# Later places for modulation rows, two retention chunk roundings, token-state remainders and the last Fourier fold

## The reference

```
mod = silu(c) @ w_ada + b_ada          # six rows of 1024: sh1, sc1, g1, sh2, sc2, g2
h   = rms_norm(x) * (1 + sc1) + sh1
u, q, k, v, g, ga, gb = split(h @ w_in)
y_four = real(fft2(u over positions and channels of 4 groups)) @ four_w_out
y_ret  = (silu(g) * group_norm(bidirectional_retention(q, k, v))) @ ret_w_out
y   = sigmoid(ga) * y_four + sigmoid(gb) * y_ret
x   = x + g1 * (y @ w_out)
h2  = rms_norm(x) * (1 + sc2) + sh2
x   = x + g2 * (square(relu(h2 @ w_mlp1)) @ w_mlp2)
out = rms_norm(x)
```

## Time and profile before

| | |
|---|---|
| median of 3 runs | 1274.28 us (1273.71 to 1274.79) |
| profiled execution, first to last instruction | 1273.3 us |
| PE busy (matmul) | 1247.7 us, 98% |
| DVE, ACT, POOL busy | 884.7, 610.2, 163.1 us |
| mean TensorE clock granted | 0.998 |

### The profile page before, as it was taken

One profiled execution on the slowest core, in us unless ns is written; L12 is line 12 of the kernel. 1 busy time (PEld: TensorE's weight loads), 2 busy tenths in 40 slices (PEclk: granted clock), 3 DMA queues, 4 the chain that ended last, 5 costly groups with the idle time before them and its releaser, 6 DMA issues.

```text
span 1273.3 us, 16935 instructions
## 1 busy us (share of the span) xinstructions
PE 1247.7 (98%) x6216; PEld 1030.8 (81%) x6216; DVE 884.7 (69%) x1392; ACT 610.2 (48%) x1039; POOL 163.1 (13%) x112
## 2 busy tenths in 40 slices
PE   5999999999999999999999999999999999999997
PEld 3788788888988878888888888888888888888886
DVE  5572577758659987877688665565555669768866
ACT  7761211235436433443677555555545433654444
POOL 0125330142260000025510000000000000000000
PEclk9999999999999999999999999999999999999999
DMA  9414220103276456496732644444448985477534
GB/s 368 181 33 154 78 100 2 34 20 100 69 274 230 141 202 211 161 365 234 265 133 88 200 166 143 149 164 142 140 156 281 320 292 183 159 236 256 193 105 160
DMA packets 95226, 219.18 MB, mean 172 GB/s; under 512 B 11532, under 2 KB 11932, under 8 KB 95144
## 3 DMA queue, kind: packets, MB, share of 16 engines
q1 hardware_dynamic: 82752, 182.70, 42.2%
q10 hardware_dynamic: 8728, 22.29, 4.7%
q0 software_dynamic: 3664, 13.11, 3.2%
HBM read 166.66 MB, written 51.39 MB: 171 GB/s over the span
## 4 chain that ended last, share of the span: by engine, by line
PE 81%; DVE 7%; DMA 6%; issue 2%; ACT 2%; POOL 1%; SPq 1%; ACTq 0%; DVEq 0%
PE ps L2988 13%; PE ps L2990 13%; PE ps L2989 13%; PE ps L3607 8%; PE ps L3599 8%; PE ps L3602 8%; DMA raw<-in_w_stream 3%; PE ps L3625 3%; PE ps L3437 3%; PE ps L3442 3%; PE ps L3439 3%; PE ps L3029 2%; PE ps L3071 1%; POOL ring_lo L1051 1%; PE ps L3224 1%
## 5 line engine op out<-in xcount | busy, mean ns | idle before, releaser
L2988 PE MATMUL ps<-t_hi,s_hi 128*128 128x512 f32 x392 | 153.4, 391 | 0.1
L2989 PE MATMUL ps<-t_lo,s_hi 128*128 128x512 f32 x392 | 153.1, 391 | 0.0
L2990 PE MATMUL ps<-t_hi,s_lo 128*128 128x512 f32 x392 | 153.1, 391 | 0.0
L1792 ACT ACTIVATE s_hi<-s_raw 128x512 fp32r<-128x512 f32 x112 | 70.5, 630 | 114.0 <-DMA b<-in_w_stream 58.4
L1051 POOL TENSOR_TENSOR ring_lo<-raw,ring_hi 128x1024 fp32r<-128x1024 f32 (+2 forms) x37 | 86.2, 2342 | 207.1 <-ACT ring_hi L1177 203.4
L2867 DVE TENSOR_TENSOR s_lo<-s_raw,s_hi 128x512 fp32r<-128x512 f32 x112 | 77.3, 690 | 42.3 <-ACT s_hi L1792 41.8
L2988 PE MATMUL ps<-ring_hi,hT_hi 128*128 128x512 f32 x224 | 91.4, 408 | 0.0
L2990 PE MATMUL ps<-ring_hi,hT_lo 128*128 128x512 f32 x224 | 87.7, 391 | 0.0
L2989 PE MATMUL ps<-ring_lo,hT_hi 128*128 128x512 f32 x224 | 87.5, 391 | 0.0
L2988 PEld LDWEIGHTS ps<-t_hi,s_hi 128*128 128x128 f32 x392 | 73.6, 188 | 16.2 <-DVE t_lo L2871 0.5
L2990 PEld LDWEIGHTS ps<-t_hi,s_lo 128*128 128x128 f32 x392 | 73.7, 188 | 15.9
(11 more groups left out here) (509 smaller groups left out, 3201.7 us busy)
## 6 DMA issues: line engine op xcount, KB each, us to landing
s_raw<-ff_scr SPq DMA_DIRECT2D x112, 256.0 KB, 2.8
raw<-in_w_stream SPq DMA_DIRECT2D x34, 512.0 KB, 3.9
ff_scr<-ffs SPq DMA_DIRECT2D x16, 1024.0 KB, 4.8
t_raw<-in_w_stream SPq DMA_DIRECT2D x64, 256.0 KB, 3.4
w_B_raw<-in_w_stream SPq DMA_DIRECT2D x48, 256.0 KB, 2.8
ff_scr<-ffa SPq DMA_DIRECT2D x16, 768.0 KB, 4.5
b<-in_w_stream SPq DMA_DIRECT2D x48, 256.0 KB, 4.5
ada_next<-in_ada_columns POOLq DMA_DIRECT2D x13, 512.0 KB, 3.8
```

Source lines behind the costliest of these rows:

```text
L1792: A(s_slot[n][0][:], s_slot[n][2][:], ACT.Copy).then_inc(down_hi, 1)
L2988: M(dst, lhsT=l_hi, rhs=r_hi, start=first, stop=False, skip_group_check=goes_on)
L2989: M(dst, lhsT=l_hi, rhs=r_lo, start=False, stop=False, skip_group_check=goes_on)
L2990: return M(dst, lhsT=l_lo, rhs=r_hi, start=False, stop=last, skip_group_check=goes_on)
```

## The change

Order and places change; no arithmetic does.

- PE: `ret_product(3)` comes before `fold(3)`. The wait of `parts(0)` for u chunk 3 moves to kt = 6. The 16 `xq` matmuls are no longer spread over the eight steps but follow the last step, in a new function `quarter_row`.
- DVE: the remainder of u chunk 3 comes behind `xq` and `operand_lo(0)` to `(2)`. `add_row(0)` and `add_row(1)` stand after the tiles m = 5 and 6, no longer 2 and 6. `add_row(7)` moves from the end of the step before j = 2 to behind `g_add("22", 2)`.
- ACT: `operand_hi(2)` comes before the rounding of u chunk 3. The load of row 1 is issued right behind that of row 0, into the second `yr_out` buffer. The roundings of re chunks 2 and 3 move from m = 3 and 4 to m = 5 and 6. The wait for both rows in front of `copy_half(8)` is split: row 0 there, row 1 in front of `copy_half(10)`.
- POOL: the two pieces of the token-state remainder (line 1116) come behind the remainders of all four "fo" chunks, no longer behind the second.

```diff
--- before.py
+++ after.py
@@ -326,7 +326,7 @@
         an = place("an", o_t + 10304, [P, 2 * EVEN - 2], F32R)
         yr_out = [place("yr_out0", o_t + 12384, [P, SEQ]), place("yr_out1", o_t + 16480, [P, SEQ])]
         gate_row = place("gate_row", o_t + 6144, [KT, P])
-        ada_first = [yr_out[0], yr_out[0], place("ada_first2", o_t + 6144, [P, D])]
+        ada_first = [yr_out[0], yr_out[1], place("ada_first2", o_t + 6144, [P, D])]
         ada_next = place("ada_next", o_qt + 12288, [P, D])
         ada_late = [place(f"ada_late{n}", o_v + 4096 * n, [P, D]) for n in range(3)] + [ada_next]
 
@@ -549,6 +549,8 @@
 
             if j == 0:
                 eng.wait_ge(dft_done, 4)
+            elif j == 1:
+                yr_stored(eng, 3)
             elif j < 18:
                 eng.wait_ge(mod_done, j)
             elif j < 21:
@@ -1108,14 +1110,14 @@
                 lo(i)
             pool.wait_ge(f_used, 10)
             nc.gpsimd.memset(wn_raw[:], 0.0).then_inc(cleared, 1)
-            for i in range(INDEX[("cs", 3)], INDEX[("fo", 2)]):
+            for i in range(INDEX[("cs", 3)], INDEX[("re", 2)]):
                 lo(i)
             pool.wait_ge(f_sum, 9)
             for n in range(2):
                 ks = slice(4 + 2 * n, 6 + 2 * n)
                 nc.gpsimd.tensor_tensor(hT_lo[:, ks, 0:512], h_raw[:, ks, 0:512], hT_hi[:, ks, 0:512].bitcast(F32),
                                         ALU.subtract).then_inc(h_whole, 1)
-            for i in range(INDEX[("fo", 2)], INDEX[("wo", 0)]):
+            for i in range(INDEX[("re", 2)], INDEX[("wo", 0)]):
                 lo(i)
             for j in range(3, 16):
                 load_ada(pool, j)
@@ -1406,9 +1408,9 @@
             operand_hi(0)
             copy_half(2)
             operand_hi(1)
+            operand_hi(2)
             hi_to(("u", 3))
-            for n in (2, 3):
-                operand_hi(n)
+            operand_hi(3)
             for r in (3, 4):
                 copy_half(r)
             for n in (4, 5):
@@ -1501,6 +1503,7 @@
             act.wait_ge(rows_stored, 16)
             act.dma_start(silu_row[:], silu_scr[0:1, :].to_broadcast([P, D])).then_inc(silu_in, 16)
             load_ada(act, 0)
+            load_ada(act, 1)
 
             def copy_b(m):
 
@@ -1519,11 +1522,9 @@
                     store_yf(m - 1)
                 if m in (1, 2):
                     hi_to(("fo", m + 1))
-                if m in (3, 4):
-                    hi_to(("re", m - 1))
-                if m == 3:
-                    load_ada(act, 1)
-            act.wait_ge(mod_done, 2)
+                if m in (5, 6):
+                    hi_to(("re", m - 3))
+            act.wait_ge(mod_done, 1)
             copy_half(8)
             store_yf(KT - 1)
             load_ada(act, 2)
@@ -1531,6 +1532,7 @@
             copy_half(9)
             g_his(1, ("B11",))
             g_his(0, ("T3", "T1"))
+            act.wait_ge(mod_done, 2)
             copy_half(10)
             g_s_hi("g1", g1_hi[:], g1_raw[:])
             g_his(1, ("T3", "T1"))
@@ -2325,12 +2327,13 @@
             even_operand(0, 1)
             for s_ in range(2):
                 even_operand(1, s_)
-            u_lo(3)
             do.chain(V.tensor_tensor(xq_raw[:, :, None], h_raw[:, :, 256:257], h_raw[:, :, 768:769], ALU.add))
             do.chain(V.tensor_copy(xq[:, :, 0:1], xq_raw[:, :, None]))
             V.tensor_tensor(xq[:, :, 1:2], xq_raw[:, :, None], xq[:, :, 0:1].bitcast(F32), ALU.subtract).then_inc(f_sum, 1)
-            for n in range(4):
+            for n in range(3):
                 operand_lo(n)
+            u_lo(3)
+            operand_lo(3)
 
             for half in range(2):
                 dve.wait_ge(f_used, 4 + half + 1)
@@ -2501,8 +2504,8 @@
                 do(V.tensor_copy(y[:, HALF:HALF + 1], ps[:, b, 256:257]))
                 do.chain(V.tensor_tensor(y[:, SEQ - 1:HALF:-2], ps[:, b + 1, 0:256], b_sb[:, 256:512], ALU.add),
                          four_free)
-                if m in (2, 6):
-                    add_row(m // 4)
+                if m in (5, 6):
+                    add_row(m - 5)
                 if m >= 6:
                     g_sums(m - 6, ("T3", "T1"))
 
@@ -2559,6 +2562,8 @@
             for j in range(1, KT - 3):
                 if j > 1:
                     g_add("22", j)
+                if j == 2:
+                    add_row(7)
                 g_los(j + 1, LATER_UNITS[2:])
                 if j < 3:
                     add_row((5, 8)[j - 1])
@@ -2570,7 +2575,8 @@
                 g_los(j + 2, LATER_UNITS[:2])
                 both_parts(j)
                 g_add("11", j + 1)
-                add_row(6 + 2 * j if j > 1 else 7)
+                if j > 1:
+                    add_row(6 + 2 * j)
             g_add("22", 5)
             g_los(6, LATER_UNITS[2:])
             g_add("12", 5)
@@ -3285,13 +3291,27 @@
             ret_product(1)
             fold(2)
             ret_product(2)
+            ret_product(3)
             fold(3)
-            ret_product(3)
             ret_product(4)
 
+            def quarter_row(cols_):
+
+                pe.wait_ge(f_sum, 5)
+                n_cols = GROUPS * (cols_.stop - cols_.start)
+                for kt in range(KT):
+                    w = slice(kt % 2 * 512, (kt % 2 + 1) * 512)
+                    for e, x in enumerate(chunk(("u", kt // 2))):
+                        r = x[:, w].rearrange("p (g d) -> p g d", g=GROUPS)[:, :, cols_]
+                        mm = M(ps[0:2, 5, 0:n_cols], lhsT=xq[:, kt, :], rhs=r, start=kt == 0 and e == 0,
+                               stop=kt == KT - 1 and e == 1)
+                return mm
+
             def parts(base, cols_, tiles):
 
                 for kt in range(KT):
+                    if kt == 6:
+                        pe.wait_ge(split, INDEX[("u", 3)] + 1)
                     w_hi, w_lo = chunk(("u", kt // 2))
                     w = slice(kt % 2 * 512, (kt % 2 + 1) * 512)
                     r_hi, r_lo = (x[:, w].rearrange("p (g d) -> p g d", g=GROUPS)[:, :, cols_] for x in (w_hi, w_lo))
@@ -3302,10 +3322,8 @@
                         l_hi, l_lo = e_operand(s_)
                         toks = slice(tile * P, (tile + 1) * P)
                         mm = mm3(ps[:, n, 0:n_cols], l_hi[:, kt, toks], l_lo[:, kt, toks], r_hi, r_lo, kt == 0, kt == KT - 1)
-                    if base == 0:
-                        pe.wait_ge(f_sum, 5)
-                        M(ps[0:2, 5, 0:n_cols], lhsT=xq[:, kt, :], rhs=r_hi, start=kt == 0, stop=False)
-                        mm = M(ps[0:2, 5, 0:n_cols], lhsT=xq[:, kt, :], rhs=r_lo, start=False, stop=kt == KT - 1)
+                    if kt == KT - 1 and base == 0:
+                        mm = quarter_row(cols_)
                     if kt % 4 == 3 or base and kt % 2 == 1:
                         mm.then_inc(f_used, 1)
 
@@ -3313,7 +3331,6 @@
             side_out(pe, ("rt", 7))
             for n in (6, 7):
                 main_read(pe, MIDX[("g", n)])
-            pe.wait_ge(split, INDEX[("u", 3)] + 1)
             parts(0, slice(0, FW), ((0, 0), (0, 1), (1, 0), (1, 1)))
             for r in (5, 6):
                 ret_product(r)
```

## The result

The changed kernel takes 1277.07 us at the median, against 1274.86 us for the kernel before on the same chip: ratio 1.0017, interval 1.0009 to 1.0024. On a second chip the two stood at 1275.75 and 1273.13 us, ratio 1.0019 (1.0010 to 1.0028). So the change costs 2.2 to 2.6 us. I had predicted a gain of 1.5 us and a range up to 1274.8. The profiled execution has a span of 1274.7 us.

The account below looks back on a forecast made before the run. PE, busy 98% of the span, was taken as the bound. Fold -1.14, Fourier -2.1, retention +0.2 and gate stage +1.5 gave -1.54 us: span 1271.8, plus 0.98 around it, 1272.7 us; range 1270.7 to 1274.8.

Parts of the forecast that it names:

- Bound and places: Whole kernel: PE busy 98% of the span; five places where it stands still hold together 5.0 us, the most to win.
- Fold and first parts: Before fold(3) and parts(0): waits for DVE remainders shrink, gain 1.14 us, bounds 0 and 1.26.
- Fourier products: Before four_product(5) and (6): both stalls go, gain 2.1 us; later retention products give back 0.2 us.
- The lock: DVE and POOL share a port pair exclusively; add_row(0) and (1) collide again with POOL's remainders, supporting the 0.2 us stall.
- Gate stage: Moving add_row(7): (3,2) gains 0.40 us, but later loads 8 and 9 delay (3,3); cost 1.5 us, bounds -0.4 and +4.
- Rival 2: Gate stage: loads 8 and 9 each land in 5.5 to 6 us, row 9 and (3,3) 4.8 us late; 1276.0 us, chance 0.09.
- Sum: Whole kernel: -1.14 - 2.1 + 0.2 + 1.5 = -1.54 us on the span, 1271.8, plus 0.98: 1272.7 us.
- Rival 1: Gate stage: the load chain absorbs the delay, row 9 late by 0.5 us or less; about 1271.2 us, chance 0.24.
- Rival 3: Early stages: parts(0) or a Fourier product meets another late operand, half of 3.2 us stays; 1274.2 us, chance 0.12.

Follow-up runs that it names:

- the rows spread: Changed kernel with rows 5 and 6 in group 1, 7 and 8 in 2, 9 to 11 in 3, 12 to 14 in 4: 1270.21 us, ratio 0.9975.
- row 7 alone: Kernel before with only the move of add_row(7) behind g_add("22", 2): 1279.78 us, ratio 1.0041.
- the two with copies: Changed kernel, row 7 at its old place, three or five plain DVE copies ahead of row 10: 1276.27 us (ratio 1.0014) and 1277.88 us (1.0027).
- the variant with early roundings: Changed kernel with the roundings of re chunks 2 and 3 back at their old places: 1276.97 us, ratio 1.0028.

## Why the prediction was wrong

**Bound and places.** TensorE is the bound, and its standing still is what moved, in one profile with a stretch of low clock behind it. Right. The 0.98 us that I added for what lies around the span is not that: in all runs with both figures the time is 1.8 us above the span (1276.53 and 1274.7 in the changed kernel's profile). So the execution that I read took about 1275.1 us (an estimate), 0.8 above its median; adding 0.98 was still the right step from that profile to the median.

**Fold and first parts.** Predicted 1.14 us; the stretch is 1.1 to 1.2 us shorter in every profile that has these edits. Both brackets went, as said. The runs with these edits alone show a gain of 0.6 us, and their interval, from a gain of 1.8 to a loss of 0.5, holds the 1.14.

**Fourier products.** Both brackets are gone. Before product 6 three of the four profiles without these edits have none either, so the edit's effect there isn't shown. The size of the term was wrong: 2.1 us was read from an execution with an unusual load wait (4.37 us, ordinarily 1.6), and 0.98 was to be had. The part of the edit that was meant for the unusual half, the late roundings, cost 0.4 to 1.1 us of the stretch (the last by 45.76 against 44.63 with the rows spread). I had 0.2 for that. My path was right (store of tile 7, ACT's copies, retention product 14), its length wasn't. In the changed kernel's ACT timeline the first rounding of a gate weight behind that store shows an idle time of 3.28 us:

```profile
384.00 0.33 ACTq L1517 DMA_DIRECT2D yf_scr<-yf_out  x1
384.42 0.39 ACTq L564 DMA_DIRECT2D ada_first<-in_ada_columns  x1
384.86 0.63 ACT L1464 ACTIVATE g_B_hi<-g_B_raw 128x512 fp32r<-128x512 f32 x1 [3.28 <-DMA g_B_raw<-in_w_stream]
```

The store itself is at 384.00, 3.0 us behind the start of the copy ahead of it (0.3 before the change), so this wait is DVE's tile 7 and not the DMA that the bracket names. The two losses in the retention products were 0.35 and 0.48 us. Of the net 1.9 us expected in this stretch 0 to 0.3 came.

**The lock.** Row 0 took 2.97 us: POOL's remainder ran from 373.64 for 2.40 us, and the row ended at 377.13, 1.09 behind it. So my reading that both late rows collide again held (row 1 took 1.86 beside the next remainder, which took 2.69 in place of 2.40). Without the late roundings row 1 took 1.23, and row 0 still 2.97. The rule of the Trainium skill (SBUF — State Buffer, section "SBUF: two separate sides") agrees with these rows, and the 0.2 that I hung on it was too small.

**Gate stage.** This step failed. I passed the delay of row 7, 1.46 us, one for one through two loads at the landing times of the profile, and got +1.5; product (3,3) was late by 2.95. In the prediction's own terms, measured from the first gate product: row 7 ended 1.96 us later, load 8 took 1.63 longer (5.32 for 3.69) and load 9 0.64 less (3.94 for 4.58), together 2.95. The first two are the terms that I had too small, and load 8 is the larger miss. At its new place it lands in 5.32, 4.95 and 5.14 us (changed kernel twice, row 7 alone), at its old place in 3.69 to 3.94 in eight profiles. I had named the reason, that it stands behind two other transfers, but took "not less" for the price. The profiles bear the reason out: with the rows spread, load 8 is issued behind three transfers of SyncE and lands in 6.42 and 6.49 us; and the tile load of SyncE takes 4.71 to 5.28 us behind load 8 and 3.43 to 3.96 ahead of it. No run changes that order alone, so other causes beside it aren't ruled out. The other miss is row 7's end. Nothing was gained at (3,2), where I had 0.40: row 6 waited 2.12 us for its load where it had waited 1.68, so `g_add("22", 2)` came 55.60 us after the first gate product, 55.49 before. That wait goes from 1.66 to 2.35 us over the profiles with this order, so the profile that I read had one of the shortest. To that came the clock, 1.45 us, in one of the two profiles, which I had not thought of. Rival 2 was the mechanism, with a chance of 0.09; its 4.8 us of delay were too many for (3,3) itself (2.95), since only one of the two loads was slow, and near the whole cost of the stage where the clock fell too (4.4); that nearness is chance, as rival 2 knew nothing of the clock. Its objection, that no row shows such a landing, used rows of loads that were issued ahead of the traffic, not behind it.

**Sum.** For the changed kernel against the second profile of before the three stretches give -1.15, -0.14 (mean of two) and +2.9 to +4.4, so +1.6 to +3.1 us; the runs say +2.2 to +2.6. Rival 1 was half right: load 9 did land in 3.94 and 3.90 us, and its 4.58 before was the longest of any profile with row 7 early; but load 8 took longer by more. Rival 3 had the right sign for the Fourier stretch but not its reason; there was less to win.

**What stays open.** In which executions the clock falls. Of the four profiles with row 7 late, rows 8 and 9 right behind it and a full load 8, two had the low clock behind the stall before (3,3) (2.94 and 2.65 us, against 2.73 and 2.53), and none of the two with copies did (1.84 and 3.21). Its share of the medians isn't measured. Open too is why row 7 alone lost 5.2 us where its profile shows 2.9.

## What to carry to other kernels

A load that waits for the reader of its buffer makes a chain of landings, and the point to look at is not when a link runs but what is queued behind it on its engine: give each link the distance of a landing, and keep the ones that may wait away from the work that the bound engine needs next. A load issued behind other transfers has to be priced above the landing times of loads issued ahead of them. Before a stall is counted as a gain, a second profile of the same kernel should show it; one here held a stall of 1.2 us that three of the four profiles of the same code didn't.

## What the runs showed of the hardware

- The granted clock fell to 0.50 for some 3 us (0.88, 0.50 and 0.76 in successive windows of the variant with early roundings, 0.84, 0.50 and 0.81 in the changed kernel) after TensorE had stood for 2.65 and 2.94 us, but stayed at 1.00 after 2.73, 2.53 and 3.21 us at the same place. The length of the stall alone doesn't decide it. The cost was 1.45 us in the changed kernel.
- The same load of 512 KB from POOL's queue, load 8, landed in 3.69 to 3.94 us when it was issued ahead of SyncE's transfers (eight profiles), in 4.95 to 5.32 behind two of them (five profiles) and in 6.42 and 6.49 behind three. SyncE's tile load lost as much by standing behind load 8: 4.71 to 5.28 us against 3.43 to 3.96.
- A load of 64 KB (128 columns of 128 partitions) landed 3.48 us after its issue, at a place where the whole 512 KB took 4.95 and 5.32 us. Seven eighths of the bytes were worth 1.5 to 1.8 us. The Trainium skill (DMA: Bandwidth & Descriptors, section "Anatomy of one DMA") makes that 2.15 and 3.2 us, an estimate from its formula: both landings here are longer, and the difference is larger than its 1.05.
- A plain copy of 128x1024 f32 on DVE came every 0.72 us (3.59 for five), against 1.22 us for the two-input operation of that size.
